# A chunked two-direction scan on one core: a column of ones beside the values, and scores kept for the second direction

## The reference, cut to what matters

```python
b = jnp.cumsum(lf, axis=-1)
logd = jnp.where(tril, b[..., :, None] - b[..., None, :] + li[..., None, :], -jnp.inf)
s = jnp.einsum('bhjd,bhsd->bhjs', qc, kc) * jnp.exp(logd - m_row[..., None])
num = jnp.einsum('bhjs,bhsv->bhjv', s, vc) + w_inter[..., None] * jnp.einsum('bhvd,bhjd->bhjv', cmat, qc)
den = jnp.sum(s, axis=-1) + w_inter * jnp.einsum('bhd,bhjd->bhj', nvec, qc)
h = num / jnp.maximum(jnp.abs(den), jnp.exp(-m_row))[..., None]
kw = kc * jnp.exp(log_in - m_new[..., None])[..., None]
cmat = carry_scale[..., None, None] * cmat + jnp.einsum('bhsv,bhsd->bhvd', vc, kw)
nvec = carry_scale[..., None] * nvec + jnp.sum(kw, axis=-2)
```

## Time and profile before

| | before |
|---|---|
| median of three runs | 3460.76 us |
| lowest, highest | 3458.69, 3464.58 us |
| the profiled execution: own time | 3454.87 us |
| its span | 3453.1 us |
| granted TensorE clock, mean over the span | 0.937 |
| PE busy | 91% of the span |
| DVE busy | 56% |
| ACT busy | 34% |

### The profile page before, as it was taken

One profiled execution on the slowest core, in us unless ns is written; L12 is line 12 of the kernel. 1 busy time (PEld: TensorE's weight loads), 2 busy tenths in 40 slices (PEclk: granted clock), 3 DMA queues, 4 the chain that ended last, 5 costly groups with the idle time before them and its releaser, 6 DMA issues. The chain is left out here.

```text
span 3453.1 us, 69128 instructions
## 1 busy us (share of the span) xinstructions
PE 3150.2 (91%) x30200; PEld 2617.6 (76%) x30200; DVE 1926.2 (56%) x3106; ACT 1170.8 (34%) x2171; POOL 319.7 (9%) x196
## 2 busy tenths in 40 slices
PE   4999799978999989988897899999988999988898
PEld 1777488867888877776796788787777777878777
DVE  3134645453677741243278588625766854766854
ACT  2111344434222231223333433324435243525442
POOL 1232000001344400032000000000000000000000
PEclk6999899987999999889798899998989999989999
DMA  7563000020111111111000122231210222210122
GB/s 265 186 231 115 2 4 5 5 81 31 61 61 61 67 55 61 54 41 63 1 1 7 57 96 93 90 104 62 74 38 4 74 92 75 80 50 4 56 86 80
DMA packets 62760, 230.30 MB, mean 67 GB/s; under 512 B 7456, under 2 KB 7968, under 8 KB 62240
## 3 DMA queue, kind: packets, MB, share of 16 engines
q1 hardware_dynamic: 62496, 226.36, 19.0%
HBM read 224.24 MB, written 2.10 MB: 66 GB/s over the span
## 5 line engine op out<-in xcount | busy, mean ns | idle before, releaser
L1787 DVE SCALAR_TENSOR_TENSOR arena<-arena,vec 128x512 f32<-128x512 f32 (+1 forms) x220 | 203.3, 941 | 25.5 <-DVE arena L1785 0.2
L357 PE MATMUL bank<-h_high_ffn,w_high_ffn 128*128 128x256 f32 x704 | 183.4, 343 | 9.6 <-DVE h_low L572 9.4
L2425 DVE SCALAR_TENSOR_TENSOR x_all<-arena,vec,x_all 128x512 f32<-128x512 f32 x240 | 180.0, 750 | 10.4 <-ACT arena L2535 3.7
L357 PE MATMUL bank<-h_low,w_high_ffn 128*128 128x256 f32 x704 | 181.8, 340 | 0.0
L1845 DVE TENSOR_TENSOR ring_low<-ring,w_high_ffn 128x1024 fp32r<-128x1024 f32 x84 | 102.5, 1224 | 141.4 <-ACT w_high_ffn L1840 138.4
L357 PE MATMUL bank<-h_high_ffn,ring_low 128*128 128x256 f32 x704 | 179.9, 336 | 0.0
L357 PE MATMUL bank<-h_high_d,w_high_d 128*128 128x512 f32 x384 | 156.9, 409 | 6.4 <-DVE h_low_d L2585 6.4
L357 PE MATMUL bank<-h_low_d,w_high_d 128*128 128x512 f32 x384 | 152.9, 398 | 0.0
L357 PE MATMUL bank<-h_high_d,ring_low 128*128 128x512 f32 x384 | 152.5, 397 | 0.0
L357 PEld LDWEIGHTS bank<-h_high_ffn,w_high_ffn 128*128 128x128 f32 x704 | 132.4, 189 | 26.4 <-DVE h_low L572 7.5
L1897 DVE SCALAR_TENSOR_TENSOR arena<-arena,vec 128x512 f32<-128x512 f32 x176 | 132.4, 752 | 30.7 <-ACT arena L1858 25.3
(11 more groups left out here) (572 smaller groups left out, 8070.4 us busy)
## 6 DMA issues: line engine op xcount, KB each, us to landing
arena<-in_ada_w_dram SPq DMA_DIRECT2D x96, 512.0 KB, 5.5
ring<-in_ffn_up_dram SPq DMA_DIRECT2D x88, 512.0 KB, 3.3
ring<-in_d_branch_dram SPq DMA_DIRECT2D x56, 512.0 KB, 3.3
ring<-in_ffn_down_dram SPq DMA_DIRECT2D x48, 512.0 KB, 3.3
ring<-in_d_in_dram SPq DMA_DIRECT2D x32, 512.0 KB, 3.3
ring<-in_ab_in_dram SPq DMA_DIRECT2D x19, 512.0 KB, 7.2
ring<-in_c_in_dram SPq DMA_DIRECT2D x17, 512.0 KB, 3.3
ring<-in_d_join_dram SPq DMA_DIRECT2D x16, 512.0 KB, 3.3
```

The costliest lines, as they stand in the source:

```text
L357: ins = M.matmul(bank_of(tile % 2, seg), w[:, at], x(k, seg), start=first, stop=last)
L1787: ins = V.scalar_tensor_tensor(y, a, w(dy, dx), y, ALU.mult, ALU.add)
L2425: ins = V.scalar_tensor_tensor(y, halves2(cpad[i][:, tap:tap + LAT]), w, y, ALU.mult, ALU.add)
```

## The change

The values' buffer gets a 257th column of ones for each chunk and head. The products of weighted keys and values are taken over 257 columns, so the sums of the weighted keys come out as the last column, and the two products with a column of ones (L2164) go. A bank holds 512 columns, so the two halves of the product, which shared one bank, now lie in two (`b[2]` and `b[3]`), and the small results that were in `b[3][:, 0:2]` move to columns 300 and 301 there. DVE reads the sums and the products from the two banks through one view, `k_sums`.

In rounds 2 and 3 ACT copies the raw scores of the unit from the bank into a place that is free by then (the keys of the context chunks), between the wait for L2214 and the exponential. In rounds 4 and 5 PE makes no raw scores (no L2141), and DVE's L2216 reads the kept ones. One memset of the ones (128x24) is added in `mlstm_mid_dve`.

```diff
-    vtk = mroom.take(NC6 * D).rearrange("p (c f) -> p c f", c=NC6)
+    VONE = 257
+    vflat = mroom.take(NC6 * 4 * VONE)
+    vtk = vflat.rearrange("p (c h v) -> p c h v", c=NC6, h=4)
...
+    kept_scores = lambda c, h: ktk[:, h // 2, 512 * (h % 2) + P * (c - 2):512 * (h % 2) + P * (c - 1)]
...
         for h in range(4):
             V.memset(state(0, h), 0.0)
+        V.memset(vtk[:, :, :, 256:VONE], 1.0)
         link(dve, dve_step, V.memset(nvec, 0.0))
...
-            M.matmul(b[:, P:2 * P], ident[0:64, row:row + 1].to_broadcast([64, P]), RM[0:64, P * c:P * c + P],
-                     start=True, stop=True)
-            for a in range(2):
+            ins = M.matmul(b[:, P:2 * P], ident[0:64, row:row + 1].to_broadcast([64, P]), RM[0:64, P * c:P * c + P],
+                           start=True, stop=True)
+            for a in range(2 if i < 4 else 0):
                 ins = M.matmul(b[:, 0:P], kqT[:, 2 * h + a, P * (c - 2):P * (c - 1)], q_at(2 * h + a, c),
                                start=(a == 0), stop=(a == 1))
...
             for a in range(2):
-                M.matmul(b[2][:, 256 * a:256 * a + 256], kwb[u % 2][:, P * a:P * a + P], v, start=True, stop=True)
-            for a in range(2):
-                ins = M.matmul(b[3][:, 2 + a:3 + a], kwb[u % 2][:, P * a:P * a + P], ones[:, 0:1], start=True, stop=True)
+                ins = M.matmul(b[2 + a][:, 0:VONE], kwb[u % 2][:, P * a:P * a + P], v, start=True, stop=True)
...
             if c >= 2:
                 act.wait_ge(to_act)
+                if i < 4:
+                    S.activation(kept_scores(c, h), psum[4 * (u % 2)][:, 0:P], ACT.Identity)
                 S.activation(eb[u % 2], tb[u % 2], ACT.Exp, bias=ctk[:, c, 0, d, h:h + 1], scale=-1.0)\
...
-            V.tensor_tensor(stb[u % 2], b[:, 0:P], eb[u % 2], ALU.mult).then_inc(made.sem, 1)
+            scores = b[:, 0:P] if i < 4 else kept_scores(c, h)
+            V.tensor_tensor(stb[u % 2], scores, eb[u % 2], ALU.mult).then_inc(made.sem, 1)
...
-            V.scalar_tensor_tensor(nvec[:, 2 * m:2 * m + 2], nvec[:, 2 * m:2 * m + 2], csb[:, m, c:c + 1], b[3][:, 2:4],
+            k_sums = banks[:, 2048 * (u % 2) + 1024:2048 * (u % 2) + 2048].rearrange("p (a v) -> p a v", a=2)
+            V.scalar_tensor_tensor(nvec[:, 2 * m:2 * m + 2], nvec[:, 2 * m:2 * m + 2], csb[:, m, c:c + 1], k_sums[:, :, 256],
                                    ALU.mult, ALU.add)
-            ins = V.scalar_tensor_tensor(state(d, h), state(d, h), csb[:, m, c:c + 1],
-                                         b[2][:, :].rearrange("p (a v) -> p a v", a=2), ALU.mult, ALU.add)
+            ins = V.scalar_tensor_tensor(state(d, h), state(d, h), csb[:, m, c:c + 1], k_sums[:, :, 0:256],
+                                         ALU.mult, ALU.add)
```

More of the change, by code:

```diff
@@ L2039, in mlstm_mid_act @@
                 act.wait_ge(prod_act)
-                p, dst = act.tiles % 2, vtk if what == "v" else ktk
-                S.activation(dst[:, 0:2, P * n:P * n + P], psum[2 * p + 1][:, 0:256].rearrange("p (c f) -> p c f", c=2),
+                p, at = act.tiles % 2, slice(P * (n % 2), P * (n % 2) + P)
+                dst = vtk[:, :, n // 2, at] if what == "v" else ktk[:, :, P * n:P * n + P]
+                S.activation(dst[:, 0:2], psum[2 * p + 1][:, 0:256].rearrange("p (c f) -> p c f", c=2),
                              ACT.Identity, scale=scale)
-                S.activation(dst[:, 2:6, P * n:P * n + P], psum[2 * p][:, :].rearrange("p (c f) -> p c f", c=4),
+                S.activation(dst[:, 2:6], psum[2 * p][:, :].rearrange("p (c f) -> p c f", c=4),
                              ACT.Identity, scale=scale).then_inc(tile_read.sem, 1)
@@ L2150, in second @@
             pe.wait_ge(made_act)
-            v, st = vtk[:, c, 256 * h:256 * h + 256], state(d, h)
+            v, st = vtk[:, c, h], state(d, h)
             if c >= 2:
                 pe.wait_ge(made)
-                M.matmul(b[1][:, 0:256], stb[u % 2], v, start=True, stop=True)
-                M.matmul(b[3][:, 0:1], stb[u % 2], ones[:, 0:1], start=True, stop=True)
+                M.matmul(b[1][:, 0:256], stb[u % 2], v[:, 0:256], start=True, stop=True)
+                M.matmul(b[3][:, 300:301], stb[u % 2], ones[:, 0:1], start=True, stop=True)
                 for a in range(2):
@@ L2158, in second @@
                 for a in range(2):
-                    M.matmul(b[3][:, 1:2], q_at(2 * h + a, c), nvec[:, 2 * (4 * d + h) + a:2 * (4 * d + h) + a + 1],
+                    M.matmul(b[3][:, 301:302], q_at(2 * h + a, c), nvec[:, 2 * (4 * d + h) + a:2 * (4 * d + h) + a + 1],
                              start=(a == 0), stop=(a == 1))
             for a in range(2):
-                M.matmul(b[2][:, 256 * a:256 * a + 256], kwb[u % 2][:, P * a:P * a + P], v, start=True, stop=True)
-            for a in range(2):
-                ins = M.matmul(b[3][:, 2 + a:3 + a], kwb[u % 2][:, P * a:P * a + P], ones[:, 0:1], start=True, stop=True)
+                ins = M.matmul(b[2 + a][:, 0:VONE], kwb[u % 2][:, P * a:P * a + P], v, start=True, stop=True)
             ins.then_inc(prod.sem, 1)
@@ L2224, in second @@
                 dve.e.sem_inc(prod_read.sem, 1)
-                link(dve, dve_step, V.tensor_copy(den[:, 2:4], b[3][:, 0:2]))
+                link(dve, dve_step, V.tensor_copy(den[:, 2:4], b[3][:, 300:302]))
                 link(dve, dve_step, V.scalar_tensor_tensor(den[:, 0:1], den[:, 3:4], ctk[:, c, 1, d, h:h + 1], den[:, 2:3],
@@ L2305, in mlstm_out_dve @@
         h4 = hacc.rearrange("p c (h v) -> p (c h) v", h=4)
-        sq = flat(vtk)[:, 0:NL * D].rearrange("p (m v) -> p m v", v=256)
+        sq = vflat[:, 0:NL * D].rearrange("p (m v) -> p m v", v=256)
         link(dve, dve_step, V.tensor_tensor(sq, h4, h4, ALU.mult))
@@ L2327, in z_low_dve @@
         V.tensor_tensor(z_low[:, n, :], zT[:, n, :], z_high[:, n, :].bitcast(F32), ALU.subtract).then_inc(h_ready.sem, 1)
-    ysq1 = vtk.rearrange("p c f -> p (c f)").rearrange("p (k t) -> p k t", k=KD)
+    ysq1 = vflat[:, 0:KD * T].rearrange("p (k t) -> p k t", k=KD)
     droom = Room()
```

## The result

The changed kernel takes 3437.43 us (median of four runs, 3433.89 to 3438.95), the kernel before in the same set of runs 3459.73 us (3456.08 to 3464.58). The ratio is 0.9936, with an interval of 0.9924 to 0.9949. The profiled execution of the changed kernel took 3438.95 on its own time, with a span of 3437.2 and a mean granted clock of 0.939. Against the profiled execution of before (3454.87) that is 15.9 us. So two things are to be explained: 3.8 us between 12.1 and 15.9, and 6.4 us between 15.9 and the difference of the medians.

What follows compares the result with a forecast made beforehand. PE was taken to bound the scan's latent units, with DVE a close second, and loops in each lane the context units. Terms 3.6 + 3.7 + 4.6 + 0.3 - 0.1 = 12.1 us gave 3448.7 us, range 3443 to 3457.

Steps and rivals of the forecast that it cites:

- The mechanism: Second mixer's scan: PE paces the latent units; with its groups removed, DVE sets the pace and PE waits for it.
- the odd columns: Rival: 257-column or misaligned passes over `v` take twice their 0.23 us, a loss of 25 us, time 3489; chance 0.05.
- The term of rounds 2 and 3: Latent units of rounds 2 and 3: 16 x (4.22 - 3.99) = 3.7 us gained.
- DVE's loop is then 3.79 + 0.20 = 3.99 in rounds 2 and 3: Latent units: DVE's loop without the wait for PE, 3.79, plus 0.20 for ACT's copy, longer than PE's 3.79.
- x: DVE's loop in latent units: distance from L2216 to L2225 when nothing is waited for, taken as 0.24 us.
- PE would need 4.22 - 0.43 = 3.79 a unit: Latent units, rounds 2 and 3: removing L2164 saves 0.43 us of PE time; without L2141, about 3.36 in rounds 4 and 5.
- The term of rounds 4 and 5: Latent units of rounds 4 and 5: 16 x (4.22 - 3.93) = 4.6 us gained.
- The context units: Scan's 16 context units: lane loop of 2.77 instead of 3.10 us for two units, 3.6 us gained.
- the clock's rival: More PE rest keeps the clock from rising in the context units; gain shrinks to 2.9 us, time 3457.9; chance 0.07.
- if it rises at the same time: Context units: clock rises 9.35 us after the first product, gain 3.6 us; a rise after 5.8 would give about 4.6.
- the third rival: Later stages start at other times against the clock's rises, so the gain is given back; time 3456 to 3461; chance 0.06.
- The step from one execution to the median: Whole kernel: the 12.1 us gain is taken from the median 3460.76 as from the profiled 3454.87, giving 3448.7.

Runs made afterwards that it cites:

- kept scores only: Kernel before, plus the score copy in rounds 2 and 3 and no raw scores in rounds 4 and 5, without the column of ones: 3447.70 us against 3460.64 (0.9968).
- ones only: Changed kernel without the kept scores: raw scores in all latent units, no copy on ACT; 3434.65 us against 3460.64 for the kernel before (0.9925).
- reordered: Changed kernel with ACT's exponential and copy ahead of the key weighting and DVE's exponent argument made earlier: 3434.76 us against 3460.64 for the kernel before (0.9929).
- PE's order: The reordered kernel with two groups of one-column passes moved behind weighted keys times values: 3427.05 us against 3457.69 for the kernel before (0.9913).
- e6: Kernel before, unchanged, profiled again: scan 167.88 us, rest of the program 3285.0 us.
- e8: Repeat of the kernel before with the kept scores alone: 3443.92 us in its one run, scan 162.86 us.
- e12: Changed kernel without an edit, timed again: 3437.33 us against 3455.58 for the kernel before (0.9943), scan 151.38 us.

## Why the prediction was wrong, point by point

**The mechanism held.** DVE became the bound in rounds 4 and 5 and PE waits for L2222 there; four 257-column passes stand in the profile with 1.11 us, the 256-column ones with 1.10, and a pass of scores times values, whose columns in `vtk` now begin at multiples of 257, has a median of 0.38 us before and after, so the odd columns cost nothing; DVE's L2241 still takes 0.74; the memset was 0.1 at the most. The clock of the context units didn't fall: its mean is 0.87 and not 0.82.

**The term of rounds 2 and 3 was mis-sized** (3.7 forecast, 5.3 measured: 16 x 0.33). The step of the prediction that failed is "DVE's loop is then 3.79 + 0.20 = 3.99 in rounds 2 and 3". The copy costs 0.16 (kept scores only), not 0.20, and x is 0.21, not 0.24: DVE's loop is 3.91. The estimate of 0.20 for the copy, worked out from the figures of the Trainium skill ("ScalarE: Activation LUTs", "What ACT_TABLE_LOAD costs"), is thus 0.04 above these rows. And x isn't the 0.34 that the prediction took from the rule of the Trainium skill ("VectorE: DVE Perf Modes", "The DRAIN you can't avoid"): L2231 starts 0.21 behind the start of an L2222 that lasts 0.29. The prediction left out that the same section has an exception, "A next op that is not held starts earlier"; with it the section and these rows don't contradict each other.

**The step "PE would need 4.22 - 0.43 = 3.79 a unit" failed too**, but by luck without a consequence for the sum. PE needs 3.89 (ones only, reordered), since the spread row loses 0.1 behind a 257-column group (PE's order). It comes out level with DVE's 3.91. The same with 3.36, which is 3.44.

**The term of rounds 4 and 5** (4.6 forecast, 5.3 measured): "2.86 + 0.83 + 0.24 = 3.93" is 2.85 + 0.83 + 0.21 = 3.89.

**The context units** (3.6 forecast, 4.4 measured). The lane loop was right at 2.78 (the loop of before is 3.10 by the rows; the clock's rival has 3.11, which changes nothing). What failed is the choice "if it rises at the same time", of the clock: the rise came 5.8 us after the first product, and for that case the prediction had 4.6. It wasn't chance, and it wasn't idle time that made the difference, since PE shows no idle time between the first product and the rise in either kernel (9.36 of 9.36 us busy before, 5.84 of 5.84 now, both at 0.50): in all ten profiled executions of kernels without the group of ones the rise came 5.1 to 6.1 us after the first product, and in all eight with it after 9.3 to 12.0 us, whatever pause stood elsewhere. Why is not shown.

Together the scan brings 4.4 + 10.5 = 14.9 us in the profiled pair (15.4 by the means), against 12.1. The forecast had named the fast ends of these very terms and put the sum of them at 14.9 with the range's lower bound; the terms that it took nearer their middle all came out at about that end. Below this sum the bound had only "some 3 us for the spread of the runs", and it was there that the range was too short: the difference of the medians goes 7.4 us beyond it.

**Outside the scan** the forecast had nothing. One part can be read. In the output stage PE starts 14.2 us after DVE in both kernels, but the clock rises 6.0 us after that start in the kernel before and 3.8 in the changed one. The windows of the kernel before, from 2 us after PE's start on:

```profile
1876.93:1880.93 4.00, 4.00 (x21) 4.00 (x20) 3.70 (x7) 1.26 (x2) 0.00 (x0) 0.50 0.00 0
1880.93:1882.93 2.00, 1.75 (x14) 1.45 (x13) 1.97 (x4) 0.63 (x1) 0.00 (x0) 1.00 0.00 0
```

and of the changed kernel, from 2 us after PE's start on:

```profile
1862.63:1866.63 4.00, 3.75 (x25) 3.48 (x23) 3.70 (x7) 1.26 (x2) 0.00 (x0) 0.78 0.00 0
```

A rise 2.2 us earlier gives back half of that, 1.1 us. In three of the four executions of before it was at 6.0 (in e6 at 4.0); in the changed kernel's three, at 3.8, 3.3 and some 4 us. That is the kind of thing the third rival had in mind, with the other sign and a smaller size. And most of it is lost again: the first product of L1815, in the stages behind, stands 100.9, 100.9, 101.0 and 100.9 us after the output stage's first operation in the kernel before and 100.4, 101.0 and 100.4 in the changed one, 0.3 us on the mean.

**The step from one execution to the median** was the last to fail: "it stands 5.89 under the median of three, 3460.76, from which I take the same 12.1". The profiled pair differs by 15.9 and the medians of the same runs by 22.3. Repeated, the medians differ by 20.7 and 18.3, and all runs together by 19.1 +- 0.9. So of the miss of 11.3 us, 2.8 lie in the scan, 1.0 beside it in the profiled pair, 1.0 in the median of before (3460.76 in the first set, 3459.73 in the second), and the remaining 6.4 lie between the profiled pair and the medians; the repeats give back about 3 of them. What remains open is the difference between 19.1 +- 0.9 and the 15.4 of the scan with 0.3 for the first 100 us behind it, some 3.4 us. It isn't particular to this change: by the means of all runs the kernel with the kept scores alone gains 10.6 +- 1.2 where its scan gains 5.0, and the one with the column of ones alone 22.8 +- 1.2 where its scan gains 15.4; for the reordered one it is 24.0 +- 1.5 and 22.6. So 1 to 7 us lie outside the scan in the edited kernels (in the reordered one within its error), and the cause stays open.

What the traces do show is where executions of the same code differ. Behind the scan, the granted clock of windows of 20 us adds up to between 153.5 us at half clock (e8, where this part lasts 1581.9) and 189.1 us (e12, 1591.6); over all eighteen profiled executions the part's length rises with that time (correlation 0.90). But its mean is 177 us for the four executions of before and 178 us for the changed kernel's three, so it doesn't explain the difference between the two.

## What to carry to other kernels

When the first bound goes, work out the second engine's loop from its own rows, and then ask what the removed instructions had been covering: four one-column passes looked like 0.43 us of work and were worth 0.33, because without them two groups follow each other that cost 0.1 us more as neighbours. Two savings on one engine don't add up when another engine's loop lies just under both; here one edit brought all of the gain, and the other became worth 7.2 us of scan only after the vector engine's round trip to the scalar engine was laid beside other work. And a gain that is worked out from one stage should be read in that stage: the stage repeated within 0.3 us where the clock rose at the same time (and within 1.3 us where it didn't), while the difference of medians for the same two kernels came out as 22.3, 20.7 and 18.3.

## What was unexpected of the hardware

A 64-row weight load behind a group of 128-row passes with 257 columns stood idle for 0.33 us and started its product 1.04 us after that group's start (1733.51 to 1734.55); behind a one-column group it shows no idle time, and reordering alone took 0.11 us off each unit (3.89 to 3.78).

The clock rose earlier after a rest, not later, when PE had less to do: 5.1 to 6.1 us after the first product without the one-column passes, 9.3 to 12.0 with them, in eighteen executions.

A multiplication on DVE whose follower reads other data lets it start after 0.21 of its 0.29 us, in the units shown, and ACT's 128-column copy from a bank, which shows 0.26 us, holds its follower back by 0.15 to 0.16.
